# A long convolution's x0 projections, moved out of the filter stage and into the transform and spectral stages

## The chip, the cores and the metric

The kernel runs on one core of a Trainium2 chip. A core has five engines that each run their own list of instructions in order: TensorE (PE, matmul; its weight loads are PEld), VectorE (DVE), ScalarE (ACT), GpSimd (POOL) and SyncE (SP, which here only issues transfers). They meet at semaphores. Transfers go through DMA queues, one behind each issuing engine (SP's is q1, ACT's is q10), and all share 16 DMA engines. The metric is the device time of one execution in microseconds (us), smaller is better. A few words return below: SBUF is the on-chip memory of 128 partitions, PSUM the smaller one that TensorE writes, DRAM the memory off the core.

## The reference, cut to what matters

The program is a Hyena block, a gated feed-forward block and a gated linear attention block on 1024 tokens of width 1024. The change touches the Hyena mixer alone:

```
z = short_conv(u @ w_in + b_in, conv_w, conv_b)      # 3 * 1024 columns, width-3 convolution
x0, x1, v = jnp.split(z, 3, axis=-1)
s = v * x1
g = hyena_filter(L, ...)                             # 2048 taps per channel, normalised by sum |g|
y = irfft(rfft(s, n=2L) * rfft(g, n=2L))[:L]
y = (y + s * skip) * x0
return y @ w_out + b_out
```

So x0 is needed only at the very end, after the inverse transform; s and g are needed before the spectral product.

## The kernel before

**Panels.** Every large projection is done in panels of 128 output columns. SP loads a panel of weights (`wraw`, two buffers of 512 KB), POOL splits it into a high and a low part (`whi` L1025, `wlo` L1027), and PE runs 48 matmuls of 128x512 on it (`panel_mm`, L1071), so that two reduced-precision products give a float32 result. Panels have one numbering through the whole program; the buffer is the number's parity, and POOL splits panel n only when panel n-2 has been used (`panel_done`).

**The transform.** The 2048-point transform is done as 128 x 16. A filter tap row m (16 of them) is made by PE from `hbs` and `wtap` (L1150), multiplied on DVE by a decay that ACT makes (`tap`, exp, L1405), and transformed over 128 points by PE (L1158). ACT copies the result out of PSUM (`gsp`, L1434) and sends it to DRAM as `g1`. DVE adds up |tap| for the norm (L1875, L1877). The signal s goes the same way: ACT gathers two token phases (`sn`, L1418), PE transposes (L1167), ACT copies (`st`, L1449), PE transforms (L1179), DVE copies out (`sa`, L1886), SP stores to DRAM as `s1`.

**The stages around the change**, each an order written out by hand per engine:

- *mix*: 8 rounds in a loop; a round is one x0 panel and two filter tap rows. The x0 panel's result is scaled on DVE (`zp`, L1807), gets its middle term on ACT (`ca`, L1373) and its outer terms on DVE (L1813, L1815), which gives `G0`.
- *sfwd*: 8 pairs of signal rows, no panels.
- *spec*: 16 groups of 8 frequencies, each in two halves of 512 channels, so 32 halves n. Per group SP loads filter rows (`wraw<-g`, 512 KB), signal rows (`bs<-s`, 512 KB) and small matrices (`kf`, 320 KB). Per half PE does six matmuls on the filter (L1219 to L1221), three on the signal, and four passes for the inverse (L1212). ACT and DVE copy and multiply in between. ACT copies the inverse's result out (`yi`, L1458, two buffers) and sends it with a transfer (L1461) straight into `YB`, the input of the last stage.
- *inv*: PE transforms `YB` over 128 points and transposes it; DVE applies skip and x0; then the output projection begins.

**Memory.** `YB` takes the place of `H`, the normalised input that every x0 panel reads. `YB` holds one frequency per pair of partitions: a group's result, 128 rows of 2 KB for one half, goes to 8 partitions.

## Time and profile before

| | |
|---|---|
| median of 3 runs | 2641.41 us (2635.97 to 2655.18) |
| the profiled execution | 2642.06 us, its span 2640.3 us |
| PE busy | 2469.5 us, 94% |
| DVE, ACT, POOL busy | 1168.0, 653.2, 705.7 us |
| PE clock, mean over the span | 0.972 of full |
| the chain that ended last | PE 70%, of it L1071 59% |

PE is busy nearly everywhere. Its largest open stretch lies between 391.7 and 633.6 us, in sfwd and spec, where it is busy for 171 of 242 us. All times below are of this one profiled execution, in us from the span's start.

### The profile page before, as it was taken

The page shows a single profiled execution, that of the slowest core. Times are in us where ns is not written, and L with a number is a line of the kernel's source. Part 1 is how long each engine was busy: PE and PEld are TensorE (multiplying, and loading weights), DVE is VectorE, ACT ScalarE, POOL GpSimd, SP SyncE. Part 2 cuts the span into 40 slices and gives each one's busy share as a digit, 9 for nine tenths or more (in the row PEclk, how much of TensorE's full clock was granted, in tenths as well). Part 3 has the DMA queues.
Part 4 walks back from the last instruction along what each step waited for, and adds up shares of the span by engine and source line. Part 5 has one row for each costly group of instructions (what it writes and reads, how often), then busy time and mean ns, then how long its engine had stood idle before and what let it go on. Part 6 is the DMA issues. An engine that isn't in the chain of part 4 may idle for free.

```text
span 2640.3 us, 29602 instructions
## 1 busy us (share of the span) xinstructions
PE 2469.5 (94%) x11356; PEld 1979.7 (75%) x11356; DVE 1168.0 (44%) x1221; ACT 653.2 (25%) x800; POOL 705.7 (27%) x394
## 2 busy tenths in 40 slices
PE   7987997677999999999999789999999999999996
PEld 5765664443788888888888679898888787778885
DVE  7899564342623311331235693626262322430443
ACT  4102344344321100000012362626363101111011
POOL 2233112231233333333333312222212232233331
PEclk9998998898999999999999899999999999999998
DMA  4232216776111111111111120202021421211231
GB/s 190 74 126 87 81 63 218 154 172 141 32 43 46 49 51 51 48 48 48 64 48 56 48 96 25 72 24 71 27 69 48 185 91 59 64 40 60 91 120 71
DMA packets 61180, 208.11 MB, mean 79 GB/s; under 512 B 6198, under 2 KB 7928, under 8 KB 60986
## 3 DMA queue, kind: packets, MB, share of 16 engines
q1 hardware_dynamic: 46170, 161.05, 19.2%
q10 hardware_dynamic: 14944, 46.14, 5.9%
q8 instruction: 46, 0.75, 0.1%
q14 instruction: 20, 0.16, 0.0%
HBM read 162.08 MB, written 36.70 MB: 75 GB/s over the span
## 4 chain that ended last, share of the span: by engine, by line
PE 70%; DVE 3%; ACT 1%; issue 0%; ACTq 0%; DVEq 0%
PE ps L1071 59%; PE ps L476 4%; DVE T L1707 1%; PE ps L1315 1%; PE ps L523 1%; PE ps L542 1%; PE ps L505 1%; PE ps L544 1%; PE ps L543 1%; PE ps L1093 0%; DVE XN L1737 0%; PE ps L1102 0%; PE ps L447 0%; DVE X L2017 0%; DVE H L1730 0%; DVE T L1737 0%
## 5 line engine op out<-in xcount | busy, mean ns | idle before, releaser
L1071 PE MATMUL ps<-H,whi 128*128 128x512 f32 x4000 | 1088.3, 394 | 35.2 <-POOL wlo L1027 14.9
L1071 PEld LDWEIGHTS ps<-H,whi 128*128 128x128 f32 x4000 | 753.0, 189 | 208.2 <-issue 23.7
L1025 POOL CAST whi<-wraw 128x1024 fp32r<-128x1024 f32 x190 | 202.9, 1068 | 1808.7 <-issue 744.9
L1071 PE MATMUL ps<-H,wlo 128*128 128x512 f32 x2000 | 618.8, 391 | 0.0
L1027 POOL TENSOR_TENSOR wlo<-wraw,whi 128x1024 fp32r<-128x1024 f32 x194 | 490.8, 2530 | 58.3 <-ACT whi L610 43.1
L1071 PEld LDWEIGHTS ps<-H,wlo 128*128 128x128 f32 x2000 | 377.3, 189 | 79.6
L1071 PE MATMUL ps<-A,whi 128*128 128x512 f32 x1472 | 395.7, 391 | 6.4 <-DVE A L2049 4.9
L1071 PEld LDWEIGHTS ps<-A,whi 128*128 128x128 f32 x1472 | 277.0, 188 | 65.3 <-issue 5.3
L1071 PE MATMUL ps<-A,wlo 128*128 128x512 f32 x736 | 227.2, 390 | 0.0
L1071 PEld LDWEIGHTS ps<-A,wlo 128*128 128x128 f32 x736 | 138.7, 188 | 29.0
L1966 DVE TENSOR_TENSOR T<-ps,T 128x1024 f32<-128x1024 f32 x22 | 26.9, 1224 | 202.6 <-PE ps L1071 202.6
L2017 DVE TENSOR_TENSOR X<-ps,X 128x1024 f32 x24 | 29.4, 1224 | 144.7 <-PE ps L1071 142.6
L1558 ACT ACTIVATE A<-T 128x1024 f32 (+1 forms) x22 | 23.3, 1061 | 280.0 <-DVE T L1969 280.0
L1844 DVE CUSTOM_DVE_ANT_0 mprod<-mw,crep 128x1024 f32<-128x1024 f32 x48 | 86.7, 1806 | 2.5 <-DVE zp L1807 1.0
L1707 DVE TENSOR_TENSOR T<-T,T 128x1024 f32<-128x1024 f32 x40 | 68.5, 1714 | 23.1 <-ACT T L1544 11.5
L1969 DVE TENSOR_TENSOR T<-T,T 128x1024 f32<-128x1024 f32 x22 | 72.3, 3286 | 3.9 <-ACT T L1555 1.4
L1555 ACT ACTIVATE T<-T 128x1024 f32<-128x1024 f32 x22 | 23.4, 1062 | 201.6 <-DVE T L1964 201.6
L476 PE MATMUL ps<-whi,H 128*128 128x256 f32 x512 | 64.4, 284 | 5.8 <-ACT whi L610 5.8
L476 PEld LDWEIGHTS ps<-whi,H 128*128 128x128 f32 x512 | 62.5, 192 | 6.6 <-issue 6.6
L1914 DVE TENSOR_TENSOR ya<-ps,ga 128x512 f32<-128x512 f32 x32 | 22.1, 691 | 98.9 <-ACT ga L1486 81.9
L1964 DVE TENSOR_TENSOR T<-ps,T 128x1024 f32<-128x1024 f32 x22 | 26.9, 1225 | 84.7 <-PE ps L1071 73.6
L2097 DVE TENSOR_TENSOR T<-X,ps 128x1024 f32<-128x1024 f32 x8 | 9.8, 1221 | 119.6 <-PE ps L1071 119.6
(342 smaller groups left out, 2587.9 us busy)
## 6 DMA issues: line engine op xcount, KB each, us to landing
wraw<-in_panels SPq DMA_DIRECT2D x181, 512.0 KB, 3.5
mw<-in_modp SPq DMA_DIRECT2D x24, 512.0 KB, 3.5
g<-gsp ACTq DMA_DIRECT2D x16, 512.0 KB, 2.6
wraw<-g SPq DMA_DIRECT2D x16, 512.0 KB, 10.9
s<-sa SPq DMA_DIRECT2D x16, 512.0 KB, 2.6
bs<-s SPq DMA_DIRECT2D x16, 512.0 KB, 6.9
YB<-yi ACTq DMA_DIRECT2D x32, 256.0 KB
kf<-in_kfft SPq DMA_DIRECT2D x16, 320.0 KB, 7.6
```

Of the source, the lines that this page charges most:

```text
L476: last = mm(p(u)[:, t * DV:(t + 1) * DV], operand(act, a, k, (t0 + t) * P, P), w[:, :, k, :], start=(k == 0 and a == 0 and w is whi), stop ...
L505: last = mm(chunk(p(14 + dr), c), chunk(KD[dr], c), chunk(QD[dr], c), start=True, stop=True)
L523: last = mm(p(u)[:, (c % 4) * DV:(c % 4 + 1) * DV], KDT[dr][:, c, :], V[:, c, :], start=True, stop=True)
L1025: nc.gpsimd.tensor_copy(whi[:, s, :, :], wraw[:, s, :, :]).then_inc(hi_made, 1)
L1027: nc.gpsimd.tensor_tensor(wlo[:, s, :, :], wraw[:, s, :, :], whi[:, s, :, :].bitcast(F32), ALU.subtract).then_inc(split_made, 1)
L1071: last = mm(p[:, c * step:(c + 1) * step], w[:, ws, k, :], operand(act, a, k, c * step, step), start=(q == 0 and w is whi and a == 0), sto ...
L1707: V_.tensor_tensor(acc, acc, tile, ALU.add).then_inc(n.acc, 1)
L1844: i_ = V_.tensor_tensor_reduce(mprod[:, :], mw[m % 4][:, :], crep[:, w * D:(w + 1) * D], 1.0, 0.0, ALU.mult, ALU.add, macc[:, m, w:w + 1])
L1964: V_.tensor_tensor(TT[0][:, :], ps[gs][:, :], TT[3][:, :], ALU.mult).then_inc(evac[gs], 1)
L1966: V_.tensor_tensor(TT[2][:, :], ps[us][:, :], TT[3][:, :], ALU.mult).then_inc(evac[us], 1)
L1969: V_.tensor_tensor(TT[2][:, :], TT[2][:, :], TT[0][:, :], ALU.mult).then_inc(ff_prod, 1)
L2017: V_.tensor_tensor(x, ps[slot(ph, u)][:, :], x, ALU.add).then_inc(evac[slot(ph, u)], 1)
```

## The change

The eight x0 panels leave the mix stage. Four go between the signal's rows (list `SFWD`), four into the spectral stage, after groups 1, 4, 7 and 10 (`X0_AFTER`). What is left of the mix stage is called `taps` and holds the 16 filter rows alone, written out, not looped. Since the last x0 panel needs `H` until group 10, the results of groups 0 to 10 (`EARLY` is 11) can't go into `YB`. They are stored to a new DRAM tensor `y1`, and SP fetches them back in two transfers of 88 x 16 x 512 elements (2.88 MB each). Groups 11 to 15 go straight into `YB` as before.

```diff
+PAIRS = N2 // 2
+SFWD = [("panel", 0), ("norm",), ("turn", 0), ("turn", 1)]
+for _i in range(PAIRS):
+    SFWD += [("dft", _i, 0), ("dft", _i, 1)]
+    if _i in (2, 5, 7):
+        SFWD.append(("panel", (2, 5, 7).index(_i) + 1))
+    if _i + 2 < PAIRS:
+        SFWD.append(("turn", _i + 2))
+X0_SFWD = 4
+X0_AFTER = (1, 4, 7, 10)
+EARLY = X0_AFTER[-1] + 1
...
-            with pe.Fori(0, 2) as i:
-                for q in range(4):
...
+            tap_values(0)
+            tap_values(1)
+            for m in range(N2):
+                if m + 2 < N2:
+                    tap_values(m + 2)
+                tap_spread(m)
...
+            for m in range(N2):
+                if m + 2 < N2:
+                    decay_rows(m + 2)
+                tap_abs(m)
+                if m % 2:
...
+                    A_(gsp[1][:, :], ps[slot("taps", o)][:, :], ACT.Copy).then_inc(evac[slot("taps", o)], 1)
+                if m + 2 < N2:
+                    decays(m + 2)
...
+            def decays(m):
+
+                if m >= 2:
+                    act.wait_ge(aux_done, A0["taps"] + spread_job(m - 2) + 1)
+                    act.wait_ge(tabs_made, m - 1)
...
             for n in range(2 * GROUPS):
                 g, c = n // 2, n % 2
-                if n >= 2:
-                    filter_spectra(n)
+                if c and g in X0_AFTER:
+                    e = N0["spec"] + spec_panel(g)
+                    k = X0_AFTER.index(g)
+                    pe.wait_ge(split_made, e + 1)
+                    if k:
+                        pe.wait_ge(x0_ev, k)
+                    panel_mm(ps[3], e % 2, H, T, 8).then_inc(panel_done, 1)
+                if n + 1 < 2 * GROUPS:
+                    filter_spectra(n + 1)
                 pe.wait_ge(spec_lo, rows_made(n))
-
-                three(bank(c, 0), g, 0, bh[c][:, :], bl[c][:, :]).then_inc(spec_xm, 1)
+                if n:
+                    pe.wait_ge(spec_y, 2 * n)
+
+                three(bank(4), g, 0, bh[c][:, :], bl[c][:, :], None if c else panel_done).then_inc(spec_xm, 1)
                 if n:
                     inverse(n - 1)
...
+            def spec_inverse(n):
+                act.wait_ge(spec_inv, n + 1)
+                if n >= 3:
+                    act.wait_ge(y1_out[n % 3], y1_stored(n - 3))
+                A_(yi[n % 3][:, :], ps[2][:, 512:1024], ACT.Copy).then_inc(spec_ev, 1)
...
+                if g < EARLY:
+                    act.dma_start(y1.rearrange("p n t -> (p n) t")[g * P:(g + 1) * P, 512 * c:512 * c + 512],
+                                  yi[n % 3][:, :]).then_inc(y1_out[n % 3], 16)
+                else:
+                    act.dma_start(YB[8 * g:8 * g + 8, :, 512 * c:512 * c + 512], yi[n % 3][:, :]).then_inc(y1_out[n % 3], 16)
...
+            def y_back(lo, hi, c0, w, k):
+                sp.dma_start(YB[lo:hi, :, c0:c0 + w], y1[lo:hi, :, c0:c0 + w]).then_inc(x_in[k], 16)
+
             for g in range(GROUPS):
...
+                if g in (13, 14):
+                    if g == 13:
+                        sp.wait_ge(panel_done, N0["spec"] + spec_panel(X0_AFTER[-1]) + 1)
+                        for n in range(2 * EARLY - 3, 2 * EARLY):
+                            sp.wait_ge(y1_out[n % 3], y1_stored(n))
+                    y_back(0, 8 * EARLY, 512 * (g - 13), 512, g - 13)
...
+            for kind, *j in SFWD:
+                if kind == "panel":
...
+                    z_tile(ps[slot("sfwd", o)], evac[slot("sfwd", o)], turn("sfwd", o) + 1, N0["sfwd"] + j[0], j[0])
+                    if j[0] < X0_SFWD - 1:
+                        x0_conv(j[0])
```

Smaller edits go with it. |tap| moves from DVE to ACT (`tap_abs`), every second filter row's copy from ACT to DVE, and the `g1` stores from ACT's queue to SP's. The signal's rows get four buffers in place of two. The products are written over `ga` and `gb`, and PE's inverse uses one PSUM bank in place of two. The list `INV` of the last stage is reordered, with the same amount of work.

**ACT in the filter stage.** Before, one round between two x0 middle terms (`hbs` are the rows of the next tap, `tap` its decay, `gsp` the copy out of PSUM):

```order
L1434 ACTIVATE gsp0_88<-ps0 128x1024
L1436 DMA g1<-gsp0_88 128x1024
L1402 ACTIVATE hbs0_91<-hb_85 64x64 x2
L1405 ACTIVATE tap0_86<-dec_84,cst_50 128x1024
L1434 ACTIVATE gsp1_89<-ps1 128x1024
L1436 DMA g1<-gsp1_89 128x1024
L1402 ACTIVATE hbs1_92<-hb_85 64x64 x2
L1405 ACTIVATE tap1_87<-dec_84,cst_50 128x1024
L1373 ACTIVATE ca_97<-zp_95,vec_49 128x1024
```

Now, the same stretch for two filter rows (`ca` and `cb` hold |tap|):

```order
L1484 ACTIVATE hbs1_92<-hb_85 64x64 x2
L1500 ACTIVATE cb__98<-tap1_87 128x1024
L1516 ACTIVATE gsp1_89<-ps1 128x1024
L1492 ACTIVATE tap1_87<-dec_84,cst_50 128x1024
L1484 ACTIVATE hbs0_91<-hb_85 64x64 x2
L1500 ACTIVATE ca_97<-tap0_86 128x1024
L1492 ACTIVATE tap0_86<-dec_84,cst_50 128x1024
```

The next rows `hbs` now stand right behind the decay of the row before, and no panel separates the rounds.

**DVE around x0 panel 2 in the signal's transform.** The row copies out of PSUM (L2007), then the panel's tile and convolution (L1916 to L1925), then the copies of the next rows:

```order
L2007 COPY gsp0_88<-ps0 128x1024
L2007 COPY gsp1_89<-ps1 128x1024
L1916 TENSOR_SCALAR zp_95<-cst_50,vec_49 128x2
L1917 TENSOR_TENSOR zp_95<-ps2,R1_96 128x1024
L1923 SCALAR_TENSOR_TENSOR ca_97<-zp_95,vec_49,ca_97 128x1024
L1925 SCALAR_TENSOR_TENSOR G0_94<-zp_95,vec_49,ca_97 128x1024
L2007 COPY sa0_103<-ps0 128x1024
L2007 COPY sa1_104<-ps1 128x1024
```

Before, that place held nothing but copies:

```order
L1886 COPY sa0_104<-ps2 128x1024
L1886 COPY sa1_105<-ps3 128x1024
L1886 COPY sa0_104<-ps1 128x1024
L1886 COPY sa1_105<-ps2 128x1024
L1886 COPY sa0_104<-ps0 128x1024
```

The convolution, which waits for ACT, has come between two rows' copies.

**SP at the end of the spectral stage**, groups 13 to 15. Before:

```order
L919 DMA wraw_60<-g1 128x1024
L946 DMA bs1_114<-s1 128x1024
L925 DMA kf1_107<-in_kfft 128x640
L919 DMA wraw_60<-g1 128x1024
L946 DMA bs0_113<-s1 128x1024
L925 DMA kf2_108<-in_kfft 128x640
L919 DMA wraw_60<-g1 128x1024
L946 DMA bs1_114<-s1 128x1024
L925 DMA kf0_106<-in_kfft 128x640
```

Now:

```order
L960 DMA wraw_60<-g1 128x1024
L966 DMA kf1_106<-in_kfft 128x640
L999 DMA bs1_116<-s1 128x1024
L990 DMA YB_126<-y1 88x16x512
L960 DMA wraw_60<-g1 128x1024
L966 DMA kf2_107<-in_kfft 128x640
L999 DMA bs0_115<-s1 128x1024
L990 DMA YB_126<-y1 88x16x512
L960 DMA wraw_60<-g1 128x1024
L966 DMA kf0_105<-in_kfft 128x640
L999 DMA bs1_116<-s1 128x1024
```

The two fetches of `y1` stand in SP's queue ahead of all that groups 14 and 15 load.

## Rows read from the trace of the kernel before

**Rows 1.** Busy time by stretch: mix, sfwd, spec (us, busy (x) per engine, PEclk, DMA share, GB/s).
```profile
257.10:391.70 134.60, 132.12 (x456) 86.35 (x457) 85.01 (x74) 50.63 (x66) 17.02 (x10) 0.98 0.17 67
391.70:440.00 48.30, 29.57 (x145) 16.51 (x143) 25.43 (x23) 21.40 (x17) 6.72 (x4) 0.83 0.60 231
440.00:633.60 193.60, 141.14 (x416) 84.42 (x417) 76.34 (x111) 78.10 (x145) 55.12 (x32) 0.90 0.75 154
```

**Rows 2.** Waits from 440 to 634 us: total us, times, longest.
```profile
ACT yi L1458 <- DMA YB<-yi: 78.7, 22, 6.8
```

**Rows 3.** PE's timeline in mix: start us, us, instruction, idle before and its releaser.
```profile
257.17 6.55 PE L1158 MATMUL ps<-tap,cst 128*128 128x512 f32 x8 [10.56 <-DVE tap L1870]
...
352.60 3.67 PE L1158 MATMUL ps<-tap,cst 128*128 128x512 f32 x8 [0.51 <-DVE tap L1870]
355.70 1.49 PE L1071 MATMUL ps<-H,whi 128*128 128x512 f32 x4
...
367.03 3.59 PE L1150 MATMUL ps<-wtap,hbs 128*128 128x512 f32 x8
```

**Rows 4.** ACT's and DVE's timelines where the filter rows begin.
```profile
253.03 0.91 DVE L1860 MEMSET gacc<- 128x1024 f32 x1 [0.28 <-DVE mgs L1858]
...
260.98 1.02 ACT L1434 ACTIVATE gsp<-ps 128x1024 f32<-128x1024 f32 x1 [3.98 <-PE ps L1158]
262.51 0.52 ACT L1402 ACTIVATE hbs<-hb 64x64 f32<-64x64 f32 x2 [0.51 <-ACT gsp L1434]
263.06 1.25 ACT L1405 ACTIVATE tap<-dec,cst 128x1024 f32<-128x1024 f32 x1
```

**Rows 5.** Groups of instructions, 250 to 800 us: xcount, busy us, mean ns, idle before.
```profile
L1870 DVE TENSOR_TENSOR tap<-ps,tap 128x1024 f32<-128x1024 f32 x16 | 19.0, 1221 | 3.0 <-PE ps L1150 1.7 <-DVE zp L1807 1.4
L1418 ACT ACTIVATE sn<-S 128x1024 f32<-128x1024 f32 x8 | 16.0, 2025 | 0.0
L1813 DVE SCALAR_TENSOR_TENSOR ca<-zp,vec,ca 128x1024 f32<-128x1024 f32 x8 | 10.3, 1284 | 1.2 <-DVE gacc L1877 1.2
L1373 ACT ACTIVATE ca<-zp,vec 128x1024 f32<-128x1024 f32 x8 | 9.9, 1241 | 68.6 <-DVE zp L1807 68.6
```

**Rows 6.** PE's timeline in sfwd: a pair's transform and the next transposes.
```profile
413.50 1.99 PE L1179 MATMUL ps<-st,cst 64*128 64x512 f32 x8
415.42 1.09 PE L1167 MATMUL ps<-cst,sn 128*128 128x128 f32 x8
```

**Rows 7.** PE's timeline in spec: the starts of two halves, and two waits of 2 us.
```profile
453.41 0.79 PE L1219 MATMUL ps<-whi,kh 128*128 128x512 f32 x1
...
457.21 0.80 PE L1219 MATMUL ps<-whi,kh 128*128 128x512 f32 x1
...
590.65 0.79 PE L1219 MATMUL ps<-bh,kh 128*128 128x512 f32 x1 [2.02 <-DVE bl L1901]
...
602.10 0.50 PE L1219 MATMUL ps<-bh,kh 128*128 128x512 f32 x1 [2.01 <-DVE bl L1901]
```

**Rows 8.** ACT's timeline: the last two halves' copies, before their transfers.
```profile
624.47 0.60 ACT L1458 ACTIVATE yi<-ps 128x512 f32<-128x512 f32 x1 [2.72 <-DMA YB<-yi]
628.92 0.60 ACT L1458 ACTIVATE yi<-ps 128x512 f32<-128x512 f32 x1 [3.85 <-DMA YB<-yi]
```

**Rows 9.** DMA queues, 445 to 600 us: packets, MB, share of the 16 engines.
```profile
q1 hardware_dynamic: 5768, 18.42, 51.1%
q10 hardware_dynamic: 3400, 6.55, 26.6%
```

**Rows 10.** The same, 625 to 629 us: `YB<-yi` alone.
```profile
q10 hardware_dynamic: 130, 0.25, 53.7%
```

**Rows 11.** The same, 634 to 636 us: the last `YB<-yi` beside the load of `X`.
```profile
q1 hardware_dynamic: 25, 0.10, 60.9%
```

**Rows 12.** A transfer on the page: KB, us from issue to landing.
```profile
X<-in_xT SPq DMA_DIRECT2D x1, 4096.0 KB, 17.4
```

**Rows 13.** The page's costliest group on POOL: busy us, mean ns.
```profile
L1027 POOL TENSOR_TENSOR wlo<-wraw,whi 128x1024 fp32r<-128x1024 f32 x194 | 490.8, 2530 | 58.3 <-ACT whi L610 43.1
```

More of the change, by code:

```diff
@@ new lines, in tap_values, with tap_spread @@
+            def tap_values(m):
+                o = tap_job(m)
+                free("taps", o)
+                pe.wait_ge(hbs_made, m + 1)
+                for c in range(2):
+                    last = mm(ps[slot("taps", o)][:, c * 512:(c + 1) * 512], hbs[m % 2][:, :],
+                              wtap[:, c * 512:(c + 1) * 512], start=True, stop=True)
+                last.then_inc(aux_done, 1)
+            def tap_spread(m):
+                o = spread_job(m)
+                free("taps", o)
+                pe.wait_ge(evac[slot("taps", tap_job(m))], turn("taps", tap_job(m)) + 1)
+                for c in range(2):
+                    last = mm(ps[slot("taps", o)][:, c * 512:(c + 1) * 512], cc("dft_g"),
+                              tap[m % 2][:, c * 512:(c + 1) * 512], start=True, stop=True)
+                last.then_inc(aux_done, 1)
@@ L1196, in _, with tap_norm @@
-            last.then_inc(aux_done, 1)
-            for u in range(3 * PAIRS - 3, 3 * PAIRS):
+            def tap_norm():
+                o = sfwd_job("norm")
+                free("sfwd", o)
+                pe.wait_ge(tap_sum, N2)
+                for e in range(KT):
+                    last = mm(ps[slot("sfwd", o)][:, e:e + 1], gacc[:, e * P:(e + 1) * P], ones[:, 0:1],
+                              start=True, stop=True)
+                last.then_inc(aux_done, 1)
+            pe.wait_ge(const_in, 32)
@@ new lines, in _ @@
+            for kind, *j in SFWD:
+                if kind == "panel":
+                    n = N0["sfwd"] + j[0]
+                    o = sfwd_job("panel", j[0])
+                    pe.wait_ge(split_made, n + 1)
+                    free("sfwd", o)
+                    panel_mm(ps[slot("sfwd", o)], n % 2, H, T, 8).then_inc(panel_done, 1)
+                elif kind == "norm":
+                    tap_norm()
+                elif kind == "turn":
+                    turned(j[0])
+                elif j[1] == 0:
+                    forward(j[0])
@@ new lines, in _ @@
+            act.wait_ge(s_made, KT)
+            act.wait_ge(aux_done, A0["taps"] + tap_job(N2 - 1) + 1)
+            gather(0)
+            gather(1)
+            act.wait_ge(aux_done, A0["taps"] + spread_job(N2 - 1) + 1)
+            due = None
+            for kind, *j in SFWD:
+                if kind == "panel":
+                    due = j[0]
+                elif kind == "turn":
+                    i, o = j[0], sfwd_job("turn", j[0])
+                    act.wait_ge(aux_done, A0["sfwd"] + sfwd_aux("turn", i))
+                    A_(st_[i % 2][:, :], ps[slot("sfwd", o)][:, :], ACT.Copy).then_inc(evac[slot("sfwd", o)], 1)
+                    if i + 2 < PAIRS:
+                        gather(i + 2)
+                    if due is not None:
+                        o = sfwd_job("panel", due)
+                        x0_middle(evac[slot("sfwd", o)], turn("sfwd", o) + 1, due)
+                        due = None
```

425 lines of the change are left out of this document (215 added, 210 removed).

## The prediction

> **What bounds the kernel now.** I read the busy time by stretch first, then the waits of the open stretch, then the engines' timelines, and the DMA queues last. In the mix stage PE is busy for 132.1 of 134.6 us, in sfwd for 29.6 of 48.3, in spec for 141.1 of 193.6 [rows 1]. So PE bounds mix, and something else bounds the other two. In spec it is the transfer of the inverse's result into `YB`: ACT waits 78.7 us for it in 22 places [rows 2]. The last two such copies start 4.45 us apart, with nothing else moving [rows 8]. Over the stage the 32 halves take 193.6 / 32 = 6.05 us each, while PE alone needs 3.80 (the starts at 453.41 and 457.21) [rows 7]. The change fills those holes with eight x0 panels, at 367.03 - 355.70 = 11.3 us each with the slow start and about 10.9 once under way [rows 3]. PE's work stays the same. What counts is how many holes each engine's order leaves, so I price the three stages from the new order and compare the moment when the last stage begins: 633.6 us before.
>
> **Filter rows without panels.** They begin when DVE's memset ends, 253.03 + 0.91 = 253.9 [rows 4]. One multiply of 1.22 [rows 5] and one transform at the low clock (6.55 us for two, so 3.3) [rows 3] put the first transform's end near 258.6. From there each tap runs in a ring, because ACT's decay for row m+1 waits for transform m-1, the `hbs` of row m+2 stand behind that decay, PE's values of row m+2 wait for these `hbs`, and transform m stands behind the values. The ring has a transform of 1.8 and values of 1.8 (3.67 and 3.59 for two) [rows 3], a decay of 1.25 and `hbs` of 0.52 [rows 4], and some 0.15 for each of the hand-overs between ACT and PE, in sum 5.5; every second tap adds ACT's copy of 1.02 [rows 4], so the mean is about 6.05. Thirteen rings give 78.6, the last two rows have no values and take 7.5: the end is at 344.7. PE now works 3.6 of each 6.05 us, with holes of about 2 and 3 us. A hole of 2.02 us was followed by matmuls at 1.2 GHz (0.79 for the first), one of 2.01 us wasn't (0.50) [rows 7]. I add 2 us and bound it by nothing and by a stage all at 1.2 GHz, 13 x 3.6 = 47 us.
>
> The move of |tap| to ACT and of one copy to DVE costs nothing: ACT's abs runs beside PE's values, DVE is the least loaded of the three. If PE's part of the ring were shorter, DVE's chain of multiply, ACT's abs and add, 1.22 + 1.0 + 1.22 plus hand-overs, would still allow 3.8 per tap. The `g1` stores move to SP's queue, where nothing is in front of them.
>
> **Signal rows with four panels.** PE's work is 4 x 10.9 for the panels, 8 x (1.09 + 1.99) for the pairs [rows 6] and 2 for the norm, 70 us. Three holes come on top. After panel 0, PE needs the norm's PSUM slot, which DVE frees only behind its convolution, which waits for ACT: transposes, ACT's copy of 1.0, its gather of 2.0, the middle term of 1.24, two convolution steps of 1.28 with gaps [rows 5], 7 us in which PE only has one more transpose. After panels 1 and 2 the next rows' copy stands behind the same convolution: PE gets to do one or two pairs and then waits 5.5 and 2.5 us. With those, 70 + 6.7 + 5.5 + 2.5 = 84.7. After each of these holes the clock is likely low for a while; I add 4. The stage ends at 346.7 + 89 = 435.7; spec began at 440.0 [rows 1], so up to here the change gives 4 us. Bounds: 76 us (half of each hole taken up) and 100.
>
> **Spectral stage, first 22 halves.** The stores to `y1` leave from 128 partitions and have three buffers, so PE's own rate decides: 3.8 per half [rows 7], 0.3 more for the ring in which ACT copies the inverse out, then `ga` and `gb`, then `bh`, on which DVE's products wait. With a first half of 9 and four panels the inverse of half 22 ends 9 + 22 x 4.1 + 43.6 - 3 (the panels cover part of the first ring) = 140 us into the stage. The convolutions lie beside PE's next half.
>
> **The end of the stage** is where I choose. From about 138 us into it SP's queue holds one fetch of 2.88 MB, group 14's three loads (1.37 MB), the second fetch, group 15's loads. Beside transfers into `YB` the loads move 18.42 MB in 155 us, 119 GB/s [rows 9]. With one such transfer running, a load got 0.10 MB in 2 us, 50 GB/s [rows 11]; a load that overlapped it only at its start got 4096 KB in 17.4 us, 241 GB/s [rows 12]. I take 119 while results are on their way into `YB` and 241 otherwise, since a starved PE also stops these transfers. Group 14's data then needs 22 us x 119 = 2.6 MB and 7 us for the rest, and is split by 168 (POOL 3.5) [rows 13]; until it is, PE's queue holds back the inverses of halves 26 and 27. The second fetch and group 15's rows need 11 us at 119 and 12 at 241, then the split: 192. Behind that stand three inverses, at 203, and three transfers of 4.5 us into `YB` from 197: half 30 has landed at 210.5. The last stage begins at 435.7 + 210.5 = 646.2, which is **12.6 us later than before**. Bounds: if fetches move at 400 GB/s, only the ten transfers of 4.5 to 5.8 us count, 189 to 198 us; at 50 GB/s see below.
>
> The Trainium skill, *DMA: Bandwidth & Descriptors* (Why a DMA increments its semaphore by 16 and not by 1), says that a transfer uses the largest number of engines up to 16 that divides both sides' outermost sizes. For the 8 partitions of `YB` that is 8 of 16, and the 53.7% share of that transfer alone [rows 10] agrees. By the rule a fetch of 88 partitions gets 11 engines; at 11/16 of 241 GB/s (an estimate from the page) the sum would be 5 us longer. It speaks against the change.
>
> **The last stage** has the same matmuls in another order; I cost it at nothing, since its rows (PE bound before) keep ACT's and DVE's parts covered.
>
> **The sum** is 2642.1 (the profiled execution, 0.7 above the median shown) + 12.6 = 2655 us. About 1%, 26 us, is what a measurement can tell here.
>
> **Rivals.**
> - *The fetches are hidden.* If SP's queue is as fast as the stores of `s1` and the clock stays full in both first stages, the last stage begins at 344.7 + 85 + 192 = 622, 12 us sooner: 2630; if DVE's holes in the signal rows also shrink to their lower bound, 2610. For it: sfwd's stores and loads moved 231 GB/s in the mean [rows 1]. Against: every number beside a transfer into `YB` is worse. Chance 0.28, of it 0.2 faster than 1%.
> - *The fetches crawl.* The other side. If a fetch gets 50 GB/s [rows 11] while `YB` is being written, 33 us of that move 1.7 MB, and the remaining 6.8 MB of the queue go at 150 to 241 in 28 to 45 us: group 15 comes at 199 to 216, half 30 lands at 217 to 235, the kernel takes 2662 to 2680, with a longer first part 2690. It decides from a fetch of more than about 25 us. Chance 0.22.
> - *The filter stage goes at 1.2 GHz.* At 61% busy, sfwd ran at a mean clock of 0.83 [rows 1]. At that mean for the whole ring the stage takes 0.2 x 47 = 9 us more; wholly at 1.2 GHz it takes 47 more, 2700. Chance of a price above 15 us: 0.08. (The Trainium skill, *TensorE: Matmul & The Clock Gate*, Part 1, holds that the clock falls when PE is idle and comes back when it is busy; by it a ring that is 60% busy may go either way, as the two rows of 2 us do.)
> - *Forecast*: 0.42, its own range 2638 to 2672.
>
> **Chances.** Faster than 2615: 0.20 (first rival's lower part). Slower than 2668: 0.08 and most of the crawl's 0.22, with a little of the forecast's upper end, 0.30. Within 1%: 0.50. The range that leaves out 2 in 10 is 2610 to 2690.
>
> **What would show it.** In the profile after: the filter rows' transforms about 6 us apart, with `hbs` as the last thing PE's values wait for; in the signal rows three holes of PE that DVE's copy ends; `YB<-yi` gone from the waits until half 22; POOL waiting for `wraw<-g` once for group 14 and once for 15, right behind each fetch. If the fetches take under 15 us each, or the ring under 5, the forecast is too high. If PE waits in the first 22 halves for loads of `bs` or `kf`, all of it is wrong, since there I let the queue be free.

## The result, and the profile after

The changed kernel takes **2707.1 us** (2703.95 to 2710.6, 4 runs) against 2640.5 before: ratio 1.024, 95% interval 1.0205 to 1.0276. The prediction said 2655, with a range up to 2690. It was wrong by 52 us, and on the side of its rival "the fetches crawl", but not for that rival's reasons.

The profiled execution takes 2707.3 us. Its stretches answer to [rows 1]: filter rows, signal rows, spectral stage up to the copy of half 22, and the rest of that stage (us, busy (x) per engine, granted clock, DMA share, GB/s).

```profile
253.90:347.20 93.30, 60.86 (x113) 23.55 (x114) 45.89 (x38) 43.93 (x63) 0.00 (x0) 0.90 0.20 83
347.20:437.60 90.40, 74.05 (x336) 52.44 (x336) 34.24 (x32) 28.11 (x22) 10.26 (x6) 0.92 0.35 129
437.60:606.70 169.10, 147.43 (x507) 101.33 (x508) 96.75 (x101) 63.09 (x113) 63.78 (x34) 0.93 0.44 153
606.70:701.30 94.60, 38.40 (x103) 22.14 (x101) 24.97 (x28) 21.55 (x38) 14.23 (x8) 0.71 0.70 128
```

The borders come from PE's timeline: the last transform, the first spectrum, and the last stage's first matmul.

```profile
344.44 2.72 PE L1213 MATMUL ps<-tap,cst 128*128 128x512 f32 x4 [3.91 <-DVE tap L1978]
...
437.62 0.47 PE L1288 MATMUL ps<-whi,kh 128*128 128x512 f32 x1 [1.76 <-DVE zp L1917]
...
701.29 13.51 PE L1341 MATMUL ps<-YB,cst 128*64 128x256 f32 x48 [5.65 <-DMA YB<-yi]
```

| moment | before | predicted | after | after - predicted |
|---|---|---|---|---|
| last filter transform ends | | 346.7 | 347.2 | +0.5 |
| spectral stage begins | 440.0 | 435.7 | 437.6 | +1.9 |
| half 22's inverse, from the stage's start | | 140 | 169.1 | +29 |
| last stage begins, from half 22 | | 70.5 | 94.6 | +24 |
| last stage begins | 633.6 | 646.2 | 701.3 | +55 |
| profiled execution | 2642.1 | 2654.7 | 2707.3 | +52.6 |

The last stage itself was 2.5 us shorter than before. So the two first stages ended where the forecast had them (the filter rows partly by luck, as shown further down), and the whole miss lies in the spectral stage, in two parts of nearly the same size. Two groups of the page show what PE waits for (busy, mean ns, idle before and its releaser): the `hbs` copies of the filter rows' ring, and in the spectral stage DVE.

```profile
L1203 PE MATMUL ps<-wtap,hbs 128*128 128x512 f32 x64 | 40.0, 765 | 41.4 <-ACT hbs L1484 41.4
L1288 PE MATMUL ps<-whi,kh 128*128 128x512 f32 x64 | 34.8, 544 | 68.4 <-DVE kl L2011 43.0
```

Both groups hold more than one cause. Of the 41.4 us, 29.3 in 13 waits lie in the ring, and 12.1 are one wait before it begins. Of the 43.0 us, 20.1 in 8 waits lie before half 22 and belong to the first part; 21.8 us are one wait behind it that comes from a late load, the second part.

**The first part: DVE and POOL meet.** DVE's timeline inside an ordinary group (start, us, instruction, idle before):

```profile
485.95 0.69 DVE L2017 TENSOR_TENSOR bl<-bs,bh 128x512 fp32r<-128x512 f32 x1 [3.75 <-ACT bh L1562]
486.56 2.70 DVE L2011 TENSOR_TENSOR kl<-kf,kh 128x384 fp32r<-128x384 f32 x1
489.19 0.68 DVE L2048 TENSOR_TENSOR ga<-ps,ga 128x512 f32<-128x512 f32 x1
```

POOL's, in the same microseconds:

```profile
485.03 1.04 POOL L1087 CAST whi<-wraw 128x1024 fp32r<-128x1024 f32 x1 [7.95 <-PE ps L1288]
486.14 2.71 POOL L1089 TENSOR_TENSOR wlo<-wraw,whi 128x1024 fp32r<-128x1024 f32 x1
```

And PE's:

```profile
489.32 0.50 PE L1288 MATMUL ps<-whi,kh 128*128 128x512 f32 x1 [2.29 <-DVE kl L2011]
```

`kl` is a subtraction of 384 columns, which took 0.55 us in the kernel before (duration min/median/max in ns):

```profile
L1895 DVE TENSOR_TENSOR kl<-kf,kh x16: 506/551/558, 439.3 to 604.9; 128x384 fp32r<-128x384 f32 x16
```

Here it takes 2.70: POOL's `wlo` starts 0.42 us earlier and ends at 488.85, and `kl` ends 0.4 us behind that. The products `ga` and `gb`, which read PSUM, keep their 0.68. The reason for the meeting is one line of the change: before, the first matmul of a group's first inverse gave the filter buffer back to POOL; now the first matmul of its x product does, half a group earlier, and that is when ACT and DVE split the next matrices. The view of this tile shows that it is the rule:

```profile
L2011 DVE TENSOR_TENSOR kl<-kf,kh x13: 2149/2699/2754, 432.6 to 598.2; 128x384 fp32r<-128x384 f32 x13
```

Not every long `kl` holds PE up. In the four groups that follow a panel group, `kl` runs beside the panel's 10.9 us of matmuls. In the other eight PE waits (waits from 437.6 to 606.7 us: total, times, longest):

```profile
PE ps L1288 <- DVE kl L2011: 20.1, 8, 3.1
```

PE's mean granted clock over this part is 0.93.

The Trainium skill, *SBUF — State Buffer* (Who interferes with whom), says that a DVE instruction with two SBUF inputs contends with a GpSimd instruction that reads SBUF, and that the one that issues second blocks until the first has finished. The trace agrees: `kl`, with two SBUF inputs, ends 0.4 us behind `wlo`, and the products, with one input in PSUM, keep their time.

**The second part: loads behind the fetches.** SP's queue at the end of the stage (the second number is how long the issue itself took):

```profile
604.10 0.98 SPq L990 DMA_DIRECT2D YB<-y  x1
605.12 6.94 SPq L960 DMA_DIRECT2D wraw<-g  x1
612.11 2.36 SPq L966 DMA_DIRECT2D kf<-in_kfft  x1
614.51 3.11 SPq L999 DMA_DIRECT2D bs<-s  x1
617.66 3.37 SPq L990 DMA_DIRECT2D YB<-y  x1
621.08 25.46 SPq L960 DMA_DIRECT2D wraw<-g  x1
646.59 1.38 SPq L966 DMA_DIRECT2D kf<-in_kfft  x1
```

The waits from 600 to 702 us (total, times, longest) are one chain: the load of the matrices is late; ACT, DVE and PE wait for it one behind the other, twice for about 20 us.

```profile
POOL whi L1087 <- DMA wraw<-g: 65.6, 2, 38.5
ACT kh L1554 <- DMA kf<-in_kfft: 40.2, 2, 21.1
DVE kl L2011 <- ACT kh L1554: 39.9, 2, 20.9
```

A fetch with nothing beside it moves at a steady rate. This row gives the GB/s in 40 slices of the stretch 607 to 617 us; the 131 to 147 is the first fetch. No packet of ACT's queue moved before 614, although its first transfer into `YB` was issued at 607.3.

```profile
GB/s 262 262 188 139 139 139 147 139 139 147 139 131 147 139 147 139 139 139 139 147 147 139 139 139 229 229 221 197 213 229 229 213 158 152 182 115 184 125 166 141
```

2.88 MB at 139 GB/s would be 20.7 us. Beside ACT's transfers into `YB` it was slower: from 616 to 628 us SP's queue moved 0.27 to 0.33 MB in each 3 us, 90 to 110 GB/s. A load of `kf` that lands in 3.1 us in the median of the stage's first part took 27.5 behind it.

The 24 us of this part fall into two. From half 22's copy to the moment when ACT has group 15's matrices it is 63.9 us (606.67 to 670.58), where the forecast had about 50; from there to the last stage 30.7, where it had about 20. In the second piece ACT copies the last five inverses in 24.7 us (671.01 to 695.67), the mean clock is 0.72, and DVE's subtractions meet POOL again (`kl` 2.72, `bl` 2.77 and 2.73 us).

### The profile page after: what moved, and what is told of

Read it like the earlier page. It is cut to its first block, busy times and chain, and to the rows that moved or that the text cites. A ratio compares the mean times of both kernels' runs of the same rounds, so it can differ in the third digit from the quotient of the medians.

```text
span 2705.5 us, 29571 instructions
## 1 busy us (share of the span) xinstructions
PE 2481.1 (92%) x11388; PEld 1990.4 (74%) x11388; DVE 1179.1 (44%) x1213; ACT 660.4 (24%) x808; POOL 707.0 (26%) x394
## 4 chain that ended last, share of the span: by engine, by line
PE 80%; DVE 8%; issue 5%; DMA 3%; ACT 3%; SPq 0%; DVEq 0%; ACTq 0%; POOL 0%; POOLq 0%
PE ps L1133 61%; PE ps L511 4%; DVE T L1817 2%; PE ps L1203 1%; PE ps L1283 1%; DMA wraw<-g 1%; PE ps L1341 1%; PE ps L1213 1%; PE ps L1398 1%; PE ps L558 1%; DMA kf<-in_kfft 1%; DVE kl L2011 1%; PE ps L1288 1%; DVE zp L1917 1%; PE ps L1292 1%
## 5 line engine op out<-in xcount | busy, mean ns | idle before, releaser
L1133 PEld LDWEIGHTS ps<-A,whi 128*128 128x128 f32 x1472 | 277.9, 189 | 63.9 <-issue 5.3
L2103 DVE TENSOR_TENSOR T<-ps,T 128x1024 f32<-128x1024 f32 x22 | 26.9, 1224 | 202.3 <-PE ps L1133 202.3
L1288 PE MATMUL ps<-whi,kh 128*128 128x512 f32 x64 | 34.8, 544 | 68.4 <-DVE kl L2011 43.0
L1203 PE MATMUL ps<-wtap,hbs 128*128 128x512 f32 x64 | 40.0, 765 | 41.4 <-ACT hbs L1484 41.4
L1288 PEld LDWEIGHTS ps<-whi,kh 128*128 128x128 f32 x64 | 13.1, 205 | 83.1 <-DVE kl L2011 50.9
```

The source lines that it names most:

```text
L1133: last = mm(p[:, c * step:(c + 1) * step], w[:, ws, k, :], operand(act, a, k, c * step, step), start=(q == 0 and w is whi and a == 0), sto ...
L1203: last = mm(ps[slot("taps", o)][:, c * 512:(c + 1) * 512], hbs[m % 2][:, :], wtap[:, c * 512:(c + 1) * 512], start=True, stop=True)
L1288: i_ = mm(bank_, kh[g % 2][:, m, :], hi, start=True, stop=False)
```

## The experiments

Times are medians; each run's own kernel before took 2638 to 2644 us. The gains in us are differences of medians to the change's 2707.1. Times of one version spread by some 4 us to each side, and gains taken from the ratios to the own kernel before come out up to 5 us smaller, so a difference of a few us between two versions says nothing. A version without the fetches that left rows of `YB` unwritten gave no time; the version with zeros below takes its place.

**Later release of POOL's buffer.**

```diff
 inverse:      last = mm(bank(5), kf[g % 3][:, m, :], src[c][:, :], ...)
+              if c == 0 and q == 0 and g not in X0_AFTER: last.then_inc(panel_done, 1)
-three(bank(4), ..., None if c else panel_done)
+three(bank(4), ..., panel_done if c == 0 and g in X0_AFTER else None)
```

> Edit: in the spectral stage a group's filter buffer is given back to POOL one half later, at the inverse of its first half and not at its x product (groups with a panel behind them excepted). PE's, ACT's and DVE's orders stay. Theory A (two engines in each other's way): POOL's subtraction wlo now starts together with DVE's subtraction kl, which then takes 2.70 us in place of 0.55, and PE's next spectra wait for kl; 7 of the first 11 groups are freed of it. A expects kl back at 0.55 in them, the inverse of half 22 about 7 x 2.3 = 16 us sooner (169 us into the stage becomes 153), the time 2691 us. Theory B (the ring through ACT, or the panels' vector work, makes the first 22 halves slow): kl may get shorter, but PE's hole goes to another wait; the stage's first part stays at 165 to 169 us, the time at 2703 to 2707. Theory C (the loads of kf come late): POOL's work starts later still, the first part grows by up to 10 us: 2717.

Measured: 2686.0 us (ratio to before 1.018), 21 less than the change. The tile view, ACT's copy of half 22, the stretch between the stage's start at 440.62 and that copy, and PE's waits for `kl` in it:

```profile
L2013 DVE TENSOR_TENSOR kl<-kf,kh x14: 551/552/2693, 436.0 to 590.2; 128x384 fp32r<-128x384 f32 x14
```

```profile
585.99 0.60 ACT L1578 ACTIVATE yi<-ps 128x512 f32<-128x512 f32 x1 [1.54 <-PE ps L1283]
```

```profile
440.62:585.99 145.37, 139.11 (x507) 96.21 (x508) 74.47 (x101) 63.07 (x113) 58.50 (x33) 0.98 0.52 175
```

```profile
PE ps L1290 <- DVE kl L2013: 3.8, 4, 3.2
```

The copy comes 145.4 us into the stage, 23.7 sooner: most of the first part's 29 us. The two rows of this part say where they come from. PE does the same 507 matmuls; its idle time falls from 21.7 us (169.1 - 147.4) to 6.3, which is 15.4 us and what theory A expected (16), and its busy time falls from 147.4 to 139.1 us, 8.3 more, since the mean clock rises from 0.93 to 0.98. So a hole is paid twice, as waiting and as slow matmuls behind it. Theory A holds, and B and C fall. Of the twelve `kl` in this part, seven are back at 0.55 us. The groups behind a panel were freed in part (1.39 us in place of 2.7), which costs PE nothing in either version; group 1's `kl` still takes 2.69 us and holds PE for 3.2.

**Both fetches behind group 15's loads.**

```diff
-if g in (13, 14): ... y_back(0, 8 * EARLY, 512 * (g - 13), 512, g - 13)
+if g == GROUPS - 1: ... both y_back
```

> Edit: both fetches of y1 stand behind the loads of group 15, none before them; amount and shape are the same. Theory F (what costs is that two groups' loads stand behind the fetches): PE's waits for kf vanish, the group's loads of 14 and 15 are taken at once, group 15's loads are issued near 620, the two fetches run from 621 for 2 x 20.6 = 41 us and share the engines with the last transfers into YB: the last stage begins at 665 to 675, time 2671 to 2681 us. Rival (the bytes cost, wherever they stand): last stage at 690 or later, time over 2695.

Measured: 2682.0 us, 25 less. The stage begins at 440.54, the last stage here:

```profile
676.83 13.30 PE L1341 MATMUL ps<-YB,cst 128*64 128x256 f32 x48 [20.18 <-DMA YB<-y]
```

236.3 us in place of 263.7; the time is 1 us above theory F's range. The waits for `kf` are gone, PE has one long stand, for the fetches themselves, and ACT waits 16.8 us in 4 places for transfers into `YB` that run beside them. So position is worth 25 us and the bytes keep a price.

**No fetch.** Rows 0 to 87 of `YB` get zeros from POOL, as the expectation says.

```diff
-    y_back(...)                                    # both fetches
+pool: memset(YB[0:88, :, 512 * k:512 * k + 512], 0.0)   # behind group 15's split
```

> Edit: no fetch of y1; POOL writes zeros into those 88 partitions of YB behind group 15's split (so rows 0 to 87 of the inverse's input are not what they should be), all else is as in the change. The price of the fetches. Theory F (the loads stand behind the fetches): from half 22's inverse, 169 us into the stage, the other nine halves come at the pace of the stage, 5.05 us, the last one is written 45 us later and has landed at 219 us into it; the last stage begins 44 us sooner and the time is 2663 us. Theory Y (the direct transfers of 256 KB into YB are late by themselves): ACT waits more than 10 us for them in nine places, the last stage begins at 230 or later, time 2674 or more. If neither, PE still waits 20 us for kf of groups 14 and 15: over 2695.

Measured: 2668.8 us, 38 less. ACT's copy of half 22, and PE:

```profile
604.90 0.60 ACT L1573 ACTIVATE yi<-ps 128x512 f32<-128x512 f32 x1 [3.70 <-PE ps L1280]
```

```profile
660.84 12.07 PE L1338 MATMUL ps<-YB,cst 128*64 128x256 f32 x48 [11.38 <-DMA YB<-yi]
```

From half 22 to the last stage it is 55.9 us, where the change takes 94.6. The fetches cost 38.7 us. The prediction had 70.5 us for the same stretch, so against this run it gave them 70.5 - 55.9 = 14.6. ACT waits for direct transfers in the last four halves only (11.1 us), and PE 11.4 us for the last of them: theory F holds, though the median lies 6 us above its 2663 (the profiled execution took 2664.0).

**What sets a fetch's time.** Three shapes at the old places: halves of the partitions in whole rows; 80 + 8 partitions in half rows; and the first again with `y1`'s rows 4352 bytes apart.

```diff
-y_back(0, 88, 512 * (g - 13), 512, g - 13)
+y_back(0, 44, 0, T, 0) ... y_back(44, 88, 0, T, 0)                      # first and third
+y_back(0, 80, 512 * (g - 13), 512, ...); y_back(80, 88, ...)            # second
-y1 = dram("y1", [P, N2, T])
+y1 = dram("y1", [P, N2, T + 64])                                        # third
```

> Edit: the two fetches of y1 take whole rows of 4 KB, YB's partitions 0 to 43 and then 44 to 87, in place of half rows of 2 KB of all 88; the bytes, their place in SP's queue and the engines that work (11, by the share of 0.69 that q1 shows while a fetch runs alone) are the same. A fetch runs at about 140 GB/s now, that is 12.7 GB/s for each of 11 engines or 161 ns for each descriptor of 2 KB; loads of the filter rows (4 KB each) run at about 400 GB/s over 16, also about 160 ns a descriptor. Theory D (a descriptor's price decides): a fetch takes 64 x 0.161 = 10.3 us in place of 20.6; PE's two stands of 21 us shrink to about 11 and the time falls by 20 us, to 2687. Theory B (bytes per engine or per SBUF port decide): no change, 2702 to 2710, and if 44 neighbouring partitions share fewer ports, slower.

> Edit: each fetch is made as two, partitions 0 to 79 and 80 to 87, still half rows of 2 KB, at the same places. If a transfer's engines are the largest number up to 16 that divides its partitions, the first part gets 16 and the second 8. Theory D and the engines' theory (12.7 GB/s each): 80 x 0.161 + 16 x 0.161 = 15.5 us in place of 20.6 each, the time falls by about 10 us to 2697, and the busy share of the queue while a fetch runs goes from 0.69 to near 1. Theory P (the SBUF side limits at 140 GB/s): no change, 2702 to 2710.

> Edit: as the run with whole rows (two fetches, partitions 0 to 43 and 44 to 87, 11 engines), but y1's rows lie 4352 bytes apart in DRAM, so that the packets cannot grow over 4 KB; there they were 64 KB each. Packets of 2 KB moved at 12.7 GB/s an engine, 161 ns each; loads with packets of 4 KB take about 165 ns a packet. Theory D (a packet's price decides): 64 x 0.165 = 10.6 us a fetch, loads right behind it, time 2707 - 20 = 2687 or, since the long packets of that run held up the transfers into YB, a few us less than its 2689. Theory B (12.7 GB/s an engine whatever the packet): two fetches of 20.6 us, 2702 to 2710.

Measured: 2689.3, 2695.9 and 2695.5 us, 18, 11 and 12 less. The times of the first two were as expected, the reasons only in part; the third, with 2695.5, fits neither of its theories (2687 or less, 2702 to 2710). In whole rows the packets were not 4 KB: a partition's 64 KB lie in one piece, and a transfer then moves them in a few very long packets. A version with such pieces (the second of the four below) shows 5.86 MB in 287 packets over 40 us; from 602 to 614 us 32 packets over 8 KB carry nearly all of 2.15 MB, 64 KB each:

```profile
q1 hardware_dynamic: 287, 5.86, 87.0%
```

With packets of 4 KB (third run) the slices that hold a fetch alone show 137 to 150 GB/s, hardly more than 2 KB packets at the same busy share of 0.7: theory D, a price per packet, falls. What shortened that version's first stand (ACT waits 12.9 us for `kf`, not 21.1) stays open. The fetch of 80 partitions moved 205 to 231 GB/s in most slices, and the engines' busy share went from 0.7 to near 1. Over 11 and 16 engines that is nearly the same rate per engine, 12.6 GB/s and 12.8 to 14.4. The rule of the Trainium skill, *DMA: Bandwidth & Descriptors* (Why a DMA increments its semaphore by 16 and not by 1), that gives 88 partitions 11 engines and 80 of them 16 agrees with both shares.

**The filter rows' ring.**

```diff
+decay_rows(2)
 for m in range(N2):
-    if m + 2 < N2: decay_rows(m + 2)
     tap_abs(m)
     ...
+    if m + 3 < N2: decay_rows(m + 3)
     if m + 2 < N2: decays(m + 2)
```

> Edit: in the filter rows ACT copies the hbs rows of tap m+3 ahead of the decay of tap m+2, not behind it; nothing else. The prediction had a ring through these copies: PE's values wait for hbs, which wait behind a decay, which waits for a transform. It was 5.83 us a tap in this execution (93.3 us for 16). If the ring is as described, PE's values wait for nothing, PE's 3.65 us a tap decide: 16 x 3.65 and 5 to 8 us at the ends make 63 to 66 us, 28 us less, and a full clock behind it; time 2679 us. Rival: DVE's chain (multiply, sum, half a copy: 3.1 us) or ACT (3.3 us) with the hand-overs takes the place of it: 4.5 us a tap, 75 us, time 2689. If the slow clock was the cause of the holes and not their effect, the gain is under 5 us.

Measured: 2686.3 us, 21 less, nearer to the rival's 2689 than to 2679. The last transform:

```profile
325.30 3.75 PE L1213 MATMUL ps<-tap,cst 128*128 128x512 f32 x4 [3.62 <-DVE tap L1979]
```

It ends at 329.05, 77.6 us behind the end of this version's own memset (251.46); in the change it was 97.4 (249.79 to 347.16). Two taps take 9.95 us in the ring (261.41 to 271.36), 4.97 each, above the rival's 4.5. The ring through `hbs` was as described: PE waits 1.61 us for `hbs` at every second tap only, where ACT's copy of the spectrum is still in front of it, and 0.97 us for DVE's multiply at the others.

**The convolutions in the signal rows.**

```diff
-    if j[0] < X0_SFWD - 1: x0_conv(j[0])          # right behind the tile
+    ... x0_conv(j[0])                             # behind the norm, or the next signal_rows
```

> Edit: in the signal rows DVE computes the convolution of an x0 tile behind the copy that PE waits for next (the norm's, or a pair of signal rows), not ahead of it. Takes away the two holes of PE that the prediction named, 6.20 us before the norm's slot is free and 5.16 us behind panel 1 (and one of 1 us), and the slow matmuls behind them (3.79 us for 8 in place of 1.99): 11.4 + 1 + about 3 us. If the holes are as described, the stage shrinks by 12 to 15 us and the time is 2692 to 2695 us. Rival: the next tile's convolution takes the place of the hole (DVE and ACT as bound): 2700 to 2707.

Measured: 2699.1 us, 8 less. The stage took 80.2 us (348.0 to 428.20) in place of 90.4: the holes were DVE's, and 10 of the 12 to 15 us came back. One hole of 3.84 us before a DVE copy is left, and the time lies between the two theories.

**The three orders together.** The three diffs above in one, with `decay_rows(m + 3)` also ahead of the copy of the spectrum; both fetches as in the change.

> Edit: the three repairs of order alone (POOL's split released later, hbs ahead of the decay and the copy, the x0 convolution behind the copies), both fetches as in the change. If the parts add up: 2707 - 21 (split) - 21 to 28 (taps) - 8 (convolution) = 2650 to 2657. The version with these three and the fetch in pieces of 48, 32 and 8 partitions took 2650: if this one takes the same, the pieces gained nothing; if it takes 2665 or more, they gained what was expected of them.

Measured: 2654.0 us (ratio 1.0046, 1.0031 to 1.0061), 53 less where the parts make 50. Within the spread they add up.

**Repaired orders with the fetch in pieces of rows.** Four versions.

```diff
+{12: [(0, 48)], 13: [(48, 80)], 14: [(80, 88)]}     # first (two of the orders), third (all three, 4 KB packets)
+{15: [(0, 48), (48, 80), (80, 88)]}                 # second (two of the orders)
+X0_AFTER = (0, 2, 4, 6)
+{8: [(0, 16)], 9: [(16, 32)], 10: [(32, 48)], 11: [(48, 64)], 12: [(64, 80)], 13: [(80, 88)]}   # fourth
```

> Edit: three things at once: POOL's split released later (as in the first experiment), hbs ahead of the decays (as in the fourth), and y1 fetched by whole rows in three pieces, partitions 0 to 47 behind group 12's loads, 48 to 79 behind group 13's, 80 to 87 behind group 14's. If the gains add up: 2707 - 21 - 21 = 2665, less what the fetch no longer costs. If descriptors decide (48 x 0.161 = 7.7 us, 5.2 and 2.6 us with 16, 16 and 8 engines) the loads of a group come at most 8 us late once and PE's stands of 42 us nearly vanish: 2625 to 2632, a little faster than the kernel before. If bytes decide, the pieces still take 41 us together and stand in front of loads: 2655 to 2665.

> Edit: as the run before it, but the three pieces stand behind group 15's loads. If descriptors decide, the pieces take 15.5 us, beside the last transfers into YB, and the last stage waits for them 5 to 10 us at most: 2625 to 2635. If bytes decide, they take 41 us: the third experiment's 25 us of gain and the other two's 42 add to 2640 at best, and PE waits 20 us for YB<-y before the last stage.

> Edit: five things: POOL's split released later; hbs of tap m+3 copied right after |tap| of m (ahead of the copy of the spectrum too); in the signal rows DVE's convolution of an x0 tile behind the next copies for PE; y1's rows 4352 bytes apart; the fetch in pieces of 48, 32 and 8 partitions behind the loads of groups 12, 13 and 14. Expected by the sum of the measured and worked out parts: 2707 - 21 (split) - 30 (taps) - 14 (holes) = 2642, and if a piece of 48 partitions takes 48 x 0.165 = 8 us, the loads are late by at most that and 30 to 40 us of PE's stands go: 2602 to 2612. If the bytes decide, the pieces take 29 us in all and half of them is seen: 2620 to 2630.

> Edit: as the run before, and the last four x0 panels stand behind groups 0, 2, 4 and 6 in place of 1, 4, 7 and 10, so that YB is free four groups sooner; y1 is fetched in six pieces of 16 partitions (the last of 8) behind the loads of groups 8 to 13. PE's work is the same. Theory F with D: each piece takes 2.6 us and is hidden, no load is late, what is left is the ten transfers into YB: 2595 to 2605. If pieces still hold up loads as in the run before, no gain over it.

Measured: 2658.6, 2662.4, 2650.3 and 2652.7 us. The first came out in its case for "bytes decide" (2655 to 2665); the second lies 22 us above even its worse case (2640), and the third 20 us above its worse case (2630). The fourth came out as its second case, no gain. By the ratio to its own kernel before, the third is where the orders without any new fetch are (1.0043 and 1.0046): the pieces gained nothing. The loads were still late in all four. A piece of 48 partitions ran at about 135 GB/s although all 16 engines worked, one of 16 partitions at 104 to 119. DMA of the fourth version while a piece of 16 partitions is fetched (GB/s in 40 slices, 572 to 583 us):

```profile
GB/s 223 141 164 223 209 194 89 119 149 104 119 104 104 104 119 89 119 89 104 134 104 119 104 104 119 104 89 119 89 104 134 104 119 119 134 179 164 134 209 357
```

So 1 MB needs 10 us, longer than PE's 7.6 for a group. In the second version ACT waited 39.7 us for one of its transfers into `YB`, while the long packets of the pieces ran.

**No direct results.**

```diff
+EARLY = 16
+{8: [(0, 16)], 9: [(16, 32)], ..., 13: [(80, 96)]}
+for k in range(2): y_back(96, 128, 512 * k, 512, k)     # behind the last half
```

> Edit: as the version with the last x0 panels behind groups 0, 2, 4 and 6, but no group goes straight into YB: all 16 go to y1 from 128 partitions, six pieces of 16 partitions are fetched behind the loads of groups 8 to 13 and the last 32 partitions (four groups) by two transfers behind the last half. Theory Y (transfers into 8 partitions, 4.5 us each for 256 KB and slower beside others, hold the engines): with them gone the stage is bound by PE, 9 + 32 x 3.9 + 43.6 = 177 us, and the last two transfers with their store take about 10: the last stage begins near 411 + 188 = 599, time about 2600 to 2610. Theory F (loads behind fetches, whatever the results do): the six pieces hold up loads as in the version before, the stage takes 215 to 230 us: 2635 to 2650.

Measured: 2641.8 us (ratio 0.9994, 0.9982 to 1.0006), the time of the kernel before. Theory F: the pieces still hold up loads, and the stage takes 227.6 us, in its range. It is also 11 us less than the fourth version above, so theory Y's transfers had a price too, though not the one that decides. The row of 569 to 576 us, one such piece alone:

```profile
DMA packets 198, 0.77 MB, mean 109 GB/s; under 512 B 11, under 2 KB 11, under 8 KB 198
```

**The same, fetched in slices over many partitions.**

```diff
+sp.dma_start(YB[lo:hi, m0:m1, :], y1[lo:hi, m0:m1, 0:T]).then_inc(x_in[0], 16)
+  # first:  partitions 0:80, 4 of 16 rows each, behind groups 11 to 14; 80:96 behind 15
+  # second: 0:32 behind 7 to 9, 32:64 behind 10 to 12, 64:96 behind 14 and 15
```

> Edit: as the version in which all 16 groups go to y1, but what is fetched behind the loads of groups 11 to 14 are quarters of the rows n2 of 80 partitions at once (1.3 MB each), then partitions 80 to 95 behind group 15's, and the last 32 partitions as before. Pieces of 16 partitions ran at 105 GB/s, the transfer into 8 partitions at 58 GB/s, 80 partitions of 2 KB packets at 205 to 257. Theory P (a transfer's rate grows with the partitions it goes to, about 6.8 GB/s for each up to 32): a quarter takes 5 to 6 us in place of 10, four of them 10 us less each group they stand in; last stage at 407 + 215 = 622, time 2620 to 2628. Theory B (a fetch's bytes cost the same in every shape, since the engines are full): 2638 to 2645.

> Edit: as the run before, but slices of 32 partitions and 5 or 6 of 16 rows n2 (0.66 to 0.79 MB) behind the loads of groups 7 to 12, and two of partitions 64 to 95 behind groups 14 and 15. The same 96 partitions, spread over more groups. Theory P: 32 partitions take 3.2 to 3.6 us a slice at about 215 GB/s, each group's loads, stores and slice together 8 us, the pace of PE: last stage at 407 + 195 to 205, time 2600 to 2612. Theory B: at 105 GB/s 6.2 to 7.5 us a slice, 2630 to 2645.

Measured: 2620.9 us (ratio 0.9916, 0.9898 to 0.9935) and **2612.6 us** (ratio 0.9898, 0.9876 to 0.9920). Both beat both kernels, by 0.8 and 1.0% of the kernel before, which is small but outside the intervals. Theory P's range held for the first (2620 to 2628) and was missed by less than 1 us by the second (2600 to 2612); both lie outside theory B's. In the first, 544 to 556 us, a slice of 80 partitions shows as the 218, the loads behind it as the 380 to 440:

```profile
GB/s 246 328 341 259 232 218 218 218 259 259 218 218 218 218 232 246 232 218 246 259 335 416 391 394 440 384 423 444 432 410 423 423 314 218 259 259 218 218 218 218
```

And PE in the second, where the stage had begun at 405.92:

```profile
605.89 12.11 PE L1349 MATMUL ps<-YB,cst 128*64 128x256 f32 x48 [8.58 <-DMA YB<-y]
```

It took 200 us for the stage with four panels in it, where the kernel before took 193.6 without any [rows 1], and the last stage begins 27.7 us sooner than in that kernel.

## Why the prediction was wrong

*Filter rows*: the ring was as described, but the 0.5 us is luck. The rows began 4.1 us sooner than the 253.9 that I took from the kernel before, and lasted 4.6 us longer (97.4 from the memset's end, where the forecast had 92.8). The thirteen rings took about 85 us, not 78.6. Of the six waits for `hbs` of 2.74 us, five were followed by slow matmuls (3.1 to 3.3 us for the values), and none of the seven of 1.83 us. The memset, and one wait of each kind:

```profile
248.88 0.91 DVE L1972 MEMSET gacc<- 128x1024 f32 x1 [0.28 <-PE ps L1203]
```

```profile
266.90 1.96 PE L1203 MATMUL ps<-wtap,hbs 128*128 128x512 f32 x4 [1.83 <-ACT hbs L1484]
...
273.32 3.27 PE L1203 MATMUL ps<-wtap,hbs 128*128 128x512 f32 x4 [2.74 <-ACT hbs L1484]
```

Two rings at full speed took 11.9 us; two rings with slow matmuls took 13.6, and there were five such pairs: 8.5 us for the clock, where I had put 2.

*Signal rows*: right within 1.4 us. The holes of 6.20 and 5.16 us (6.7 and 5.5 forecast) lay where DVE's order put them, a third of 2.67 us lay before panel 3, and the run with the later convolution took most of them away.

```profile
368.63 3.78 PE L1241 MATMUL ps<-st,cst 64*128 64x512 f32 x8 [6.20 <-DVE rn L2031]
...
399.22 3.79 PE L1241 MATMUL ps<-st,cst 64*128 64x512 f32 x8 [5.16 <-DVE gsp L2007]
```

*Spectral stage, first 22 halves*: the step failed. "PE's own rate decides: 3.8 per half, 0.3 more for the ring" left out a length. I took DVE's splits at their durations from a kernel in which POOL worked at another moment, and did not follow the one increment that the change moves, though the diff shows it. It cost 23.7 of the 29 us, shown by the later release: 15.4 us in which PE stood, eight times behind `kl`, and 8.3 us of slower matmuls, a price of the clock that this step had at nothing. The other 5 us stay open; group 1's `kl`, long in both versions, is 3 us of PE's waiting. The text named loads of `bs` or `kf` as what would break this step; it was neither.

*The end of the stage*: the mechanism was right (group 14's and 15's loads behind the fetches, PE's queue held by them), its size was not. The term that failed is the rate of SP's queue. I let it move 119 GB/s beside ACT's transfers and 241 without them, the fetches like the loads, from [rows 9] and [rows 12]. The fetch moved 139 with nothing beside it and 90 to 110 beside ACT's transfers. So group 15's matrices came about 14 us late. The other 10 us of the miss lie behind them, where I had put the last inverses 3.7 us apart and they came 6.2 apart. The fetches cost 38.7 us, not 14.6 (shown by the run without fetches). [rows 12] was the wrong nearest row: it goes to 128 partitions. The estimate that the prediction drew from the Trainium skill's *DMA: Bandwidth & Descriptors*, 11/16 of 241 or 166 GB/s, pointed the right way; the fetch ran at 139. The 5 us that the text put on it don't follow from its own sum either: only 1.9 MB of the fetches go at 241 there, and at 166 they take 3.5 us longer.

*The rivals*: "the fetches crawl" had the right place and side and ended at 2690. With the first part's 29 us taken out of the measured 2707, 2678 lies in its 2662 to 2680; its mechanism, 50 GB/s for a fetch beside the writes into `YB`, was not seen (90 to 110). The range failed because no case had both errors, and because nothing in the sum could make the first 22 halves dearer. At its other end the 2610 of "the fetches are hidden" doesn't follow from its terms: 9 us less for DVE's holes leave 2621. The rival of the filter stage at a low clock was right in kind, with its 9 us near the 8.5 measured.

*The last stage*: at nothing, measured 2.5 us less.

## What to carry to other kernels

When a change moves the signal that gives a buffer back, draw the other engine's work at its new time beside the critical engine's short instructions: here a 0.55 us subtraction that became 2.70 on the ring cost 24 us, a third of it through the clock. A bulk transfer in the queue that feeds the loop held up all loads behind it. What helped here was to cut it into slices that fit beside one turn's loads, and so that each slice still goes to many partitions; pieces of few partitions gained nothing. And where two steps of a sum rest on durations taken beside other neighbours, widen for both at once.

## What the runs showed of the hardware

- A DVE subtraction of 128x384 with two SBUF inputs took 0.55 us alone and 2.70 beside POOL's `wlo`, which had started 0.42 us earlier. Beside POOL's cast, which reads SBUF too, it took 1.39 us (version with the later release, 459.18 us).
- Rates into SBUF differed with the partitions that a transfer reaches: 8 partitions about 59 GB/s (256 KB every 4.45 us [rows 8]), 16 partitions 104 to 119, 32 partitions 217, 48 about 135, 80 partitions 205 to 231, 88 partitions 139, loads to 128 partitions 380 to 440. The 32 are a slice of the last version, alone from 536.4 to 537.4 us:

```profile
DMA packets 53, 0.22 MB, mean 217 GB/s; under 512 B 0, under 2 KB 0, under 8 KB 53
```

  The Trainium skill, *SBUF — State Buffer* (Door 1: The DMA port swizzle), counts ports of 27.2 GB/s each, 2 for such 8 partitions, 4 for 16, and the same 8 for partitions 0 to 31 and 0 to 63. Estimates from that page are 54, 109 and 218 GB/s for 8, 16 and 32 partitions: the runs agree. For 48 partitions the estimate is 218 too, and for 80 and 88, whose first 64 share those 8 ports, it is 272 and 300 (218 x 80/64 and x 88/64), where the runs show 135, 205 to 231 and 139: here they don't agree. The 88 ran on 11 engines and the 80 on 16, by their busy shares of 0.7 and near 1; what held back the 48 stays open.
- The issue of a DMA on SP's queue took up to 25.5 us when a large transfer was in front of it; elsewhere it took 0.3 to 0.4.
- A source that lies in one piece of 64 KB per partition was moved in packets of 64 KB, and ACT waited 39.7 us for a small transfer of its own queue while they ran; rows 4352 bytes apart brought packets of 4 KB back.
- PE's holes of 2 to 3 us in these stages were at times followed by matmuls at the lower of the two clock levels: with eight waits for `kl` of 2.3 to 3.1 us the mean granted clock was 0.93, with one such wait 0.98, and the same matmuls were busy for 8.3 us more.
